# Two fewer buffers for gathered expert rows, three query columns loaded at the block's begin, one load of the norm's row

## What is computed

```python
def peer_ffn(h, wq, sub_keys, u_table, v_table):        # h: 512 x 1024, normalised
    q = (hf @ wq).reshape(t, 8, 2, 128)                 # 16 query columns of 128
    sc = einsum('thpd,hpnd->thpn', q, sub_keys)         # scores against 128 keys each
    top_v, top_i = top_k(sc, 16)                        # per half, then 16 of 16 x 16 sums
    ...                                                 # expert_id: 8 heads x 16 per token
    gate = softmax(best_v)
    act = gelu(einsum('phkd,pd->phk', u_table[expert_id], x))
    out = einsum('phk,phkd->pd', gate * act, v_table[expert_id])
```

## Time and profile before

| | us |
|---|---|
| median of 3 runs | 2721.81 |
| lowest and highest run | 2717.55, 2721.88 |
| span of the profiled execution | 2719.8 |
| first gather issued | 1393.6 |
| last gather issued | 2682.0 |

### The profile page before, as it was taken

The page is one execution under the profiler, slowest core; times in us unless marked ns, Lnnn a source line. Parts: engine busy times, 40 slices in busy tenths (PEclk is TensorE's granted clock), DMA queues, the critical chain, the costliest instruction groups (busy, mean ns, idle before and its releaser), DMA issues.

```text
span 2719.8 us, 28480 instructions
## 1 busy us (share of the span) xinstructions
PE 2336.9 (86%) x9248; PEld 1533.5 (56%) x9248; DVE 1591.9 (59%) x3408; ACT 706.6 (26%) x1912; POOL 1487.4 (55%) x1052
## 2 busy tenths in 40 slices
PE   8999899899989988889888889888777777777776
PEld 7888678788878868767664434444233233222222
DVE  1266691434430668632278777887778777555555
ACT  2111552215421230232232222222223222111112
POOL 6777377676567743076356565565544544334331
PEclk9999999999999998989999999999999999999999
DMA  4223002222222210021169999999999999999996
GB/s 144 93 93 100 9 9 93 93 93 86 95 79 92 99 41 1 1 93 62 47 261 421 421 421 421 418 407 415 421 421 423 421 422 421 421 421 422 421 421 264
DMA packets 105899, 646.35 MB, mean 238 GB/s; under 512 B 12721, under 2 KB 15153, under 8 KB 39601
## 3 DMA queue, kind: packets, MB, share of 16 engines
q0 software_dynamic: 73728, 536.90, 47.6%
q1 hardware_dynamic: 31776, 106.87, 11.6%
q10 hardware_dynamic: 272, 1.05, 0.1%
HBM read 640.58 MB, written 4.19 MB: 237 GB/s over the span
## 4 chain that ended last, share of the span: by engine, by line
DMA 31%; PE 10%; DVE 5%; POOL 2%; issue 1%; ACT 1%; POOLq 0%; DVEq 0%
DMA peer_row<-in_peer_uv,peer_ids 31%; PE bank L3123 7%; DVE peer_row L3068 2%; PE bank L281 2%; POOL peer_row L3045 1%; PE bank L2817 1%; POOL w_parts L229 1%; ACT peer_diag L3102 1%; POOL w_parts L227 1%; DVE peer_weight L3060 1%; DVE peer_top_i L2636 0%; DVE peer_top_v L2632 0%; DVE peer_place L2636 0%; DVE peer_sc_left L2639 0%; PE bank L2778 0%
## 5 line engine op out<-in xcount | busy, mean ns | idle before, releaser
L3123 PE MATMUL bank<-peer_row,peer_diag 128*128 128x512 f32 x2048 | 965.0, 617 | 269.2 <-ACT peer_diag L3102 267.6
L3045 POOL DMA_INDIRECT peer_row<-in_peer_uv,peer_ids x512 | 580.1, 1133 | 651.8 <-PE bank L3123 611.7
L3123 PEld LDWEIGHTS bank<-peer_row,peer_diag 128*128 128x128 f32 x2048 | 379.6, 194 | 824.6 <-ACT peer_diag L3102 431.6
L3068 DVE CUSTOM_DVE_ANT_0 peer_row<-peer_row,peer_h_tok 128x1024 f32<-128x1024 f32 x512 | 639.9, 1254 | 333.7 <-DMA peer_row<-in_peer_uv,peer_ids 332.7
L208 POOL TENSOR_TENSOR w_parts<-ring,zero 128x1024 fp32r<-128x1024 f32 x156 | 295.3, 1893 | 230.8 <-PE bank L281 114.3
L211 POOL TENSOR_TENSOR w_parts<-ring,w_parts 128x1024 fp32r<-128x1024 f32 x156 | 373.5, 2394 | 29.1 <-POOL w_parts L208 29.1
L3106 ACT ACTIVATE peer_acts<-peer_dots 128x2 f32<-128x2 f32 x256 | 52.1, 204 | 739.6 <-DVE peer_dots L3068 739.6
L3102 ACT ACTIVATE peer_diag<-ident,peer_weight 128x128 f32<-128x128 f32 x512 | 177.5, 394 | 226.1 <-DVE peer_weight L3060 221.9
L257 PE MATMUL bank<-ssm_h_high,w_parts 128*128 128x512 f32 x512 | 157.9, 389 | 0.8 <-DVEq L645 0.8
L257 PEld LDWEIGHTS bank<-ssm_h_high,w_parts 128*128 128x128 f32 x512 | 96.1, 188 | 20.9 <-DVEq L645 1.0
L257 PE MATMUL bank<-hyb_h_high,w_parts 128*128 128x512 f32 x320 | 100.1, 394 | 0.8 <-DVEq L645 0.8
(11 more groups left out here) (560 smaller groups left out, 3779.1 us busy)
## 6 DMA issues: line engine op xcount, KB each, us to landing
ring<-in_weights SPq DMA_DIRECT2D x180, 512.0 KB, 3.2
peer_row<-in_peer_uv,peer_ids POOLq DMA_INDIRECT x512, 25.3
resid<-in_x SPq DMA_DIRECT2D x4, 512.0 KB, 8.1
out<-resid SPq DMA_DIRECT2D x4, 512.0 KB, 7.7
xa_mem<-in_mem ACTq DMA_DIRECT2D x1, 1024.0 KB, 5.2
xa_kept<-xa_v_out SPq DMA_DIRECT2D x1, 1024.0 KB, 6.0
xa_kept<-xa_k_out SPq DMA_DIRECT2D x1, 1024.0 KB, 3.8
xa_v<-xa_kept SPq DMA_DIRECT2D x1, 1024.0 KB, 4.7
```

Source lines behind the costliest of these rows:

```text
L3045: pool.indirect_dma_start(self.rows[row][:, :], None, self.m.ins["peer_uv"], bass.IndirectOffsetOnAxis(ap=self.choice.ids[:, t, slot:slot ...
L3068: dot = dve.tensor_tensor_reduce(mine, mine, self.tokens(slot_of(j)[0]), 1.0, 0.0, ALU.mult, ALU.add, self.dots[:, h % 4, r:r + 1])
L3123: mm = pe.matmul(self.m.banks[2 * t + half][:, :], self.diag[:, j % (2 * GROUP), :], self.rows[row][:, D + half * 512:D + (half + 1) * 512 ...
```

## The change

Seven instead of nine buffers hold rows, until row 210 instead of 207; from then on there are 12 instead of 13. In the room of two of them (74 to 90 KB of a partition, with the norm's row at 82) stand query columns 8, 9 and 10, each in a buffer of its own (`apart`). SP loads these three at the begin of the block, ahead of the output projection's units, and POOL splits them from there. The ring holds the other columns, 4 to 7 and 11 to 15. The norm's row is loaded once and stays at 82 for both pairs of tiles. Three waits differ: POOL no longer waits for the first token vectors before row 3; it waits for column 3's matmuls before row 5 and not row 6; and DVE waits for the last scores instead of the second load of the norm's row before it makes the second pair of token vectors.

```diff
-FIRST_ROWS, ROWS, SWITCH = 9, 13, 207
+FIRST_ROWS, ROWS, SWITCH = 7, 12, 210
 FIRST = 4
+APART, APARTS = 8, (74, 78, 86)
...
+    def sync_apart(self, sp):
+        for n, raw in enumerate(self.apart):
+            sp.dma_start(raw[:, :], self.m.ins["weights"][self.u0 + APART + n]).then_inc(self.apart_loaded[n], 16)
+
+    def sync_rest(self, sp):
+
+        m = self.m
+        for x in range(FIRST, HP):
+            if APART <= x < APART + len(APARTS):
+                continue
+            at = self.place(x)
...
+            sp.wait_ge(m.w_split, self.u0 + before + 1)
+            sp.dma_start(m.ring[:, at % RING, :], m.ins["weights"][self.u0 + x]).then_inc(m.w_loaded[at % RING], 16)
+
+    def gpsimd_split(self, pool, x):
+        m, u = self.m, self.u0 + x
+        if APART <= x < APART + len(APARTS):
+            raw = self.apart[x - APART][:, :]
+            pool.wait_ge(self.apart_loaded[x - APART], 16)
+        else:
+            at = self.place(x)
+            raw = m.ring[:, at % RING, :]
+            pool.wait_ge(m.w_loaded[at % RING], 16 * (at // RING + 1))
...
+            queries.sync_apart(sp)
             stream_weights(m, sp, DT)
-            sp.dma_start(gain[0][:, :], m.row("norm_ffn", D)).then_inc(gain_loaded, 16)
+            sp.dma_start(gain[:, :], m.row("norm_ffn", D)).then_inc(gain_loaded, 16)
             sp.dma_start(queries.keys[:, :, :], ins["peer_keys"]).then_inc(queries.keys_loaded, 16)
-            stream_weights(m, sp, HP)
-            sp.wait_ge(queries.scores_done, HP)
-            sp.dma_start(gain[1][:, :], m.row("norm_ffn", D)).then_inc(gain_loaded, 16)
+            queries.sync_rest(sp)
             sp.wait_ge(m.w_split, all_units)
             experts.sync(sp)
...
                 if x < HP and j == 2 * column_step(x) - 1:
-                    split_ahead(m, pool, 1)
+                    queries.gpsimd_split(pool, x)
                     x += 1
-                if j == 3:
-                    pool.wait_ge(tokens_made, 2)
-                if j == 6:
+                if j == 5:
                     pool.wait_ge(m.w_used, queries.u0 + FIRST)
...
-                    dve.wait_ge(gain_loaded, 32)
+                    dve.wait_ge(queries.scores_read, HP)
...
-        places = [74, 90, 98, 82, 106, 114, 58, 66, 8] + [H_AT + 8 * n for n in range(4)]
+        places = [90, 98, 106, 114, 8, 58, 66] + [H_AT + 8 * n for n in range(4)] + [74]
```

More of the change, by code:

```diff
@@ L2757, in __init__, with place @@
         self.parts = m.at(58, "peer_parts", [P, 2, 2, UNIT], F32R)
+        self.apart = [m.at(kb, f"peer_apart{n}", [P, UNIT]) for n, kb in enumerate(APARTS)]
+        self.apart_loaded = [sem(f"peer_apart_loaded{n}") for n in range(len(APARTS))]
+    def place(self, x):
+        return self.u0 + x - (len(APARTS) if x >= APART + len(APARTS) else 0)
+    def sync_apart(self, sp):
[7 more added lines that the diff above has]
+            at = self.place(x)
+            before = next(y for y in range(-DT, HP) if self.u0 + y - (len(APARTS) if y >= APART + len(APARTS) else 0) == at - RING
+                          and not APART <= y < APART + len(APARTS))
+            sp.wait_ge(m.w_split, self.u0 + before + 1)
[9 more added lines that the diff above has]
+            pool.wait_ge(m.w_loaded[at % RING], 16 * (at // RING + 1))
+        high, low = (m.parts[:, u % 2, n, :] for n in range(2))
+        pool.wait_ge(m.w_used, u - 1)
+        pool.tensor_tensor(high, raw, m.zero[:, :].broadcast_to([P, UNIT]), ALU.add).then_inc(m.w_high, 1)
+        pool.wait_ge(m.w_high, u + 1)
+        pool.tensor_tensor(low, raw, high, ALU.subtract).then_inc(m.w_split, 1)
     def q_bank(self, x):
@@ L2857, in peer @@
         h = [m.at(H_AT + 16 * x, f"peer_h_{y}", [P, DT, SEQ], F32R) for x, y in enumerate(("high", "low"))]
-        gain = [m.at(kb, f"peer_gain{n}", [P, D]) for n, kb in enumerate((82, 154))]
+        gain = m.at(82, "peer_gain", [P, D])
         rms = RootMean(m, c, "peer_norm", 31, 2)
@@ L2959, in tokens @@
                     t = 2 * pair + n
-                    dve.scalar_tensor_tensor(h_tok[pair][:, n, :], m.resid[:, t, :], rms.of(t), gain[pair][:, :],
+                    dve.scalar_tensor_tensor(h_tok[pair][:, n, :], m.resid[:, t, :], rms.of(t), gain[:, :],
                                              ALU.mult, ALU.mult).then_inc(tokens_made, 1)
```

## The result

The changed kernel took 2741.45 us (median of 4 runs, 2735.89 to 2744.59), the kernel before 2720.70 (4 runs): ratio 1.0077, 95% interval 1.0063 to 1.0091. It is slower by 21 us; the forecast was 2724, the range ended at 2733.

The account below looks back on a forecast made before the run. The DMA queue was taken to bound the kernel, one row per 2.48 us. Bytes -5.0, start +1.9 and splits +5.2 summed to +2.1 us; from the 2721.8 median the forecast was 2724, range 2717 to 2733.

Parts of the forecast that it names:

- The bound: In the gather stretch: the DMA delivers as fast as it can, one row per 2.48 us; only bytes or empty-queue moments count.
- Bytes taken away: In the gather stretch: three columns' units and the norm's second load leave, 2.10 MB, -5.0 us together.
- The block's begin: Ahead of the projection's first ring loads: three added loads cost 0, 3.7 us without cover; as a rival 2728, chance 0.04.
- The 13th buffer: In the later stretch: twelve buffers instead of 13 take one beat from a line of at least 20.6 us, cost 0.
- The moved waits: POOL's waits before rows 3 and 5 and DVE's wait for the last scores: cost 0.
- The start: At row 7, first to need a used buffer: issue 1415.06, landing 1420.3 against 1418.4 due, shortfall 1.9 us.
- The twelve splits: At rows 15 to 183 behind POOL's splits: 11.7 us needed from use to landing; shortfalls 3.7 plus 1.5, together 5.2 us.
- second rival: Rows 15 to 183: the line runs dry at each split, from a refill price of 6 us on; 2734 us, chance 0.25.
- refill price: For a gather with nothing ahead of it: least time from issue to landing, taken as 5.2 us, between 4.4 and 6.4.
- the ring load: A load of half a row's bytes: 3.2 us from issue to landing, giving the refill price's lower bound of 4.4.
- The upper bound, 6.4: Refill price's upper end, from row 0's landing by 1400.9 and its 1.91 us issue; would give net +12.
- The estimate of 2742: Time of the dry line at each split by the Trainium skill's 6.15 us per 1 MB, a refill price of 7.1 us.

Follow-up runs that it names:

- the later loads: Changed kernel with five ring loads and the final norm's row released by a column's last matmuls instead of its split: 2744.15 us, ratio 1.0088.
- the lone gathers: Kernel before, with POOL waiting for the previous row's landing ahead of each of gathers 300 to 331: 2854.43 us, one run.
- the absence by itself: Changed kernel with one-element splits for columns 4 to 15 and 17 small POOL instructions in front: 2745.64 us, ratio 1.0096.

## Why the prediction was wrong, by its own steps

**The bound, right.** The DMA's queue sets the time; all of the loss is in moments in which it is empty or slow, and none behind row 209.

**Bytes taken away, -5.0, right as far as the runs tell.** The seven buffers alone are 4 to 5 us slower than the change with its loads.

**The block's begin, 0, right.** The first gather goes out at 1393.66, before at 1393.58. The 13th buffer, 0: right, by the rows from 210 on. The moved waits, 0: right. The wait before row 5 holds POOL for 1.13 us where 0.30 is usual, with five rows in line:

```profile
1401.68 0.94 POOL L3080 DMA_INDIRECT peer_row<-in_peer_uv,peer_ids  x1 [1.13 <-PE bank L2855]
```

DVE goes into the second pair of token vectors with no idle time.

**The start, 1.9: mis-sized.** Row 7's issue was forecast at 1415.1, and came at 1415.20; its landing 1420.3, and came at 1421.0. Not in the sum was the second row: row 8 lost 1.2 more. Together 3.5.

**The twelve splits, 5.2: this is the step that failed.** "From that use on: 0.25 us to the issue, 0.94 for it, 5.3 for the split, and 5.2 until row j lands, together 11.7 us." The twelve rows took 12.5 to 15.5, on average 14.0. The count of waits was sound, its terms were not:

- From use to issue 6.6 to 7.2 us, on average 6.85, and not 6.5.
- From issue to landing 7.2 on average, and not 5.2. In four rows (71, 87, 135, 151) nothing but gathers moved much data beside the row: 6.2, 5.7, 6.5, 5.8, mean **6.05**. This is the price that was taken too low: 4.5 us behind the issue's end where the prediction had 4.3, and above all the issue is 1.23 or 1.84 us long there, not 0.94. The other eight have a 512 KB load (six of them) or a 16 KB instruction fetch beside them and take 7.2 to 8.3; the later loads showed that the loads cost about their bytes.
- The second row behind a dry moment can be late as well: by 1.4, 0.5, 0.9 and 1.0 us behind those four rows, by 1.2 at the start, by 1.0 behind the last of the lone gathers (3.47 us instead of 2.48). No term stood for it. It does not come at every split: rows 16, 24, 104, 168 and 184 keep the beat to within 0.15 us. Over the twelve splits it is 5.8 us.

The long issue stood in the trace of before already: of its twelve issues behind a split, eleven take 1.2 or 1.8 us, and the one shown in the earlier trace rows, 0.96, is the exception. Rows 71 and 119, before:

```profile
1573.29 1.77 POOL L3045 DMA_INDIRECT peer_row<-in_peer_uv,peer_ids  x1
1699.57 1.23 POOL L3045 DMA_INDIRECT peer_row<-in_peer_uv,peer_ids  x1
```

Put into the prediction's own list of what each split had (12.7, 15.1, 11.1, 12.8, 12.7, 13.8, 10.0, 12.8, 11.3, 11.5, 10.9, 11.6 us): with 6.85 + 6.05 = 12.9 needed, the shortfalls are 11.6, and the missing ring loads add 2.9, together 14.5. The landings say the same: the twelve rows land 22.0 us behind their beat in all, and the six loads beside them are about 7.5 of these. (The loads that are gone stood behind the splits ahead of rows 71, 87 and 103, not 87, 103 and 119 as the prediction has it; its sum of 1.5 is the same with the right rows.) The second rows add 5.8. That is 20.3 us, where 27.5 - 3.5 = 24 were measured. The remaining 4 lie in rows further behind, whose buffers came back late, such as rows 89 to 91, late by 0.5, 0.8 and 0.6 us; they are not divided up here. The prediction had no term for anything behind row j. The sum then is -5.0 + 3.5 + 24 = +22.5, by row 209.

The prediction did have this case, as its second rival: "the line runs dry at each split, from a refill price of 6 us on". The mechanism, the place and the price hold; its 2734 was too low, since it had no term for the second and the later rows. What spoke for 5.2 was the ring load, a transfer that SP issues, in 0.3 to 0.4 us by its timeline, and half as large; the issue of row 0, 1.91 us in the earlier trace rows, was read as an exception and was the better guide. The upper bound, 6.4, came from a gather and was within half a microsecond of the 5.9 and 6.05 measured. In the changed kernel row 0 has a record of its landing: 6.4 us from the start of an issue of 1.91, so 4.5 behind its end, as in the four rows above.

The Trainium skill ("DMA: Bandwidth & Descriptors", Bandwidth) has 6.15 us of DMA time for 1 MB without the issue; here a lone gather takes 4.6 us behind its issue, so the trace does not agree. The estimate of 2742 that the prediction worked out from it came near by luck: its 7.1 us from issue to landing is close to the 7.2 that the twelve rows took on average, but that mean holds the longer issues and the loads beside the gathers, and not a slower transfer. The formula on the same page (Anatomy of one DMA), 2.0 us plus the bytes at 436 GB/s, gives 4.4. That is near the 4.6 behind the issue's end; but the page counts the set-up in its 2.0 us, and from the start of the issue the trace has 5.9.

**What DVE's collision adds.** By itself nothing (nine buffers, later splits), and the absence by itself makes most of the loss. In the seven-buffer kernel both sit at the same place: moving the split gives 9 us back, halving it 13, both 14. How the 24 us divide between them has no single answer, and I leave it there. The Trainium skill ("SBUF — State Buffer", SBUF: two separate sides) says that a VectorE instruction with two inputs in SBUF and a GpSimd instruction that reads SBUF exclude each other for the whole instruction; the rows at 1628.45 and 1631.15 agree, with 1.6 and 2.1 us of wait.

## What to carry to other kernels

With a ring of buffers in front of a full queue, compare the depth of the line at its least with the longest absence of the engine that issues: the line must outlast the absence, the issue and the first landing together (here 12.9 us behind the use that frees the buffer of the gather before the absence). What is missing is paid at every such place, and what is over brings nothing. Take the price of a first landing from the same kind of transfer on the same issuing engine, add something for the second one behind it (here up to 1.4 us), and lean to the bound that stems from that kind. If a buffer must go, first cut the long instructions of the issuing engine in two and issue between the halves.

## What the runs showed of the hardware that was not expected

- A gather of 1 MB alone needs 4.6 us behind its issue, though a full line delivers one each 2.48 us; and the one behind it comes after 3.0 to 3.8 us where no load is beside the first. In a full line both are hidden. Why the first two are slow is open.
- An issue of the same gather takes 0.94 us or up to 1.9; behind the splits from row 39 on it takes 1.83 and 1.23 in turn, in the changed kernel as (but for row 103) in the kernel before. What makes it long was not tried.
- Beside the gathers run instruction fetches on queues of their own. The DMA view of the changed kernel's window 1450 to 1900 (queue, kind: packets, MB, share):

```profile
q0 software_dynamic: 23839, 173.65, 95.4%
q1 hardware_dynamic: 720, 2.62, 1.6%
q8 instruction: 8, 0.13, 0.1%
q14 instruction: 13, 0.11, 0.1%
```

Eight packets of 16 KB are next to nothing as bytes, but they cost a row some time. In the kernel before, at seven of nine such packets one row landed 0.93 to 0.97 us behind its beat, with its neighbours on theirs; in the changed kernel the same happened by up to 1.1 us.
